# Context decay sums from high and low parts, both token tiles in one product; up tiles wait for high weights first

## The chip, the cores and the metric

The kernel runs on one core of a Trainium2 chip. The metric is device time in microseconds (us) of one execution. A core has five engines with instruction queues of their own, each worked off in order: TensorE (PE; its weight loads are shown apart as PEld), VectorE (DVE), ScalarE (ACT), GpSimd (POOL) and SyncE (SP, here only a DMA queue). They meet through semaphores: an instruction adds to one when it is done, and a `wait_ge` in another engine's program holds that engine until the count is there.

## The reference, cut to what matters

The program is one layer of a hybrid transformer (attention beside gated linear attention, GLA, then an MLP) followed by a second layer (mLSTM mixer, MLP, gated embedding), for 256 tokens of width 1024. The change touches one small piece of mathematics, the state that the 256 context tokens leave for GLA, and one waiting point in the MLPs:

```python
def gla_log_decay(lowrank, w_gk, b_gk):
    g = jax.nn.log_sigmoid((lowrank @ w_gk + b_gk).astype(jnp.float32)) / GLA_GATE_NORM
    return gla_heads(g, GLA_DK)

def gla_final_state(k, v, g):
    b = jnp.cumsum(g, axis=2)
    return jnp.einsum('bhtd,bhte->bhde', k * jnp.exp(b[:, :, -1:] - b), v)

s_f = gla_final_state(kgc, vgc, gfc)
s_b = gla_final_state(flip_t(kgc), flip_t(vgc), flip_t(gbc))

def sq_relu_mlp(h, w1, w2):
    return jnp.square(jax.nn.relu(h @ w1)) @ w2
```

There are 4 GLA heads of key width 128, 256 context tokens (two tiles of 128), and a forward and a backward direction. `b_last - b` is a sum of the decays of all later tokens (earlier ones for the backward direction), so it is a product with a strict triangle of ones.

## The kernel before, in words

All large weights arrive as 278 units of 128 x 1024 numbers in a ring of four buffers (`raw`). ACT rounds each unit to fp32r, the "high part" (`w_hi`, L1392, semaphore `hi_done`); DVE subtracts it from the original, the "low part" (`w_lo`, L1911, semaphore `unit_cut`, waited for by `wait_cut`). Activations are split the same way, and a product is three fp32r matmuls: low times high, high times high, high times low (`product`, L796). A weight tile is four units.

The order of the work is written out by hand in three plans. A plan is one list of steps, and every engine walks through the whole list and issues its own part of each step. `woven(tile, side)` lays the eight pieces of a tile's matmuls (six matmuls each in this part) beside side steps; the steps `round` (ACT) and `cut` (DVE) split the next tile's units in between. In tiles `aq1` and `ga0` the order is: piece, `round` 0, `gstate 0`; piece, keys' rotary part 2, `cut` 0; piece, `round` 1, `gstate 1`; piece, `round` 2, keys' part 3, `cut` 1; piece, `gstate 2`, `cut` 2; piece, `round` 3, keys' part 4; piece, `gstate 3`, `cut` 3; piece, queries' part 0; two pieces of `ga0`, `gstate 4`; two more pieces, `gstate 5`. The rotary parts (`rope_keys`, `rope_queries`, L2135 to L2198) are DVE's.

`gla_state(j)` is the `gstate` step, a pipeline over the four heads h:

- PE: `out` of head j-2 (L1005, decayed keys times values), then `cum` of head j-1 (L1017 and L1019, the triangle sums, plain fp32 matmuls into bank 5), then the gate product of head j (L1033).
- ACT: the copy of head j-2's state (L1566), the exponential of head j-1's sums (L1573), then Abs, Exp, Ln of head j's gate (L1558 to L1560).
- DVE: the product with the keys of head j-1 (L2231, semaphore `gs_kd`), then `min(x, 0) - log` of head j (L2236, semaphore `gs_g`), which ends that head's log decays in `gs_a`.

So DVE finishes the decays of head h in step `gstate h`, and PE sums them in step `gstate h+1`, waiting for `gs_g` alone.

The MLPs (tags `a` and `b`) run eight steps each of `up` and `down` tiles. `up` (L1163, L1166) does, for each bank, eight matmuls with the high weights (512 columns: high and low activations side by side) and then eight with the low weights (256 columns). For the first bank it waits, before every second of the high matmuls, for the unit's low part (`wait_cut`).

Of the kernel before, what the change touches and what calls it, by code (L numbers as in the profile page):

```python
# [24 lines left out]
P = 128  # L25
# [362 lines left out]
QK_BLOCKS = (tuple(zip(range(4), (7, 6, 4, 5))), ((4, 7), (5, 6)))  # L388
ROOT_ON_POOL = ("n2",)
SCALED_LATER = ("n3", "n4", "n5")  # L390
AWAKE = {}
# [8 lines left out]
def build(nc, a, out):  # L400
    with ExitStack() as ctx:
# [39 lines left out]
        diag_block = sb("diag_block", [P, 32])  # L441
        gx_c = sb("gx_c", [P, 2, 2, 32])
        gx_more = sb("gx_more", [P, N_LVL - 3, 2 * T])
        stat = sb("stat", [P, 8, 16])
# [129 lines left out]
        def head_of(name, h):  # L574
# [35 lines left out]
        go_sig, gomul_done, sig_ready = sem("go_sig"), sem("gomul_done"), sem("sig_ready")  # L610
        gs_mm, gs_ln, gs_g, gs_cum, gs_exp, gs_kd, gs_out, gs_copy = (
            sem(n) for n in ("gs_mm", "gs_ln", "gs_g", "gs_cum", "gs_exp", "gs_kd", "gs_out", "gs_copy"))
        gx_mm, gx_ln, gx_g, gx_scan, gx_eq, gx_qin = (
# [9 lines left out]
        res_ready = sem("res_ready")  # L623
        hid_done, relu_done, hid_half, hid_sum, hsq_done, hhi_done, hlo_done = (
            sem(n) for n in ("hid_done", "relu_done", "hid_half", "hid_sum", "hsq_done", "hhi_done", "hlo_done"))
        down_done, acc_done = sem("down_done"), sem("acc_done")
# [5 lines left out]
                             "mg_mt", "mg_md", "mg_em"))  # L632
        pick_zero = sem("pick_zero")
        pick_ready, mg_hi, mg_lo, mh_bc, mh_arg, mh_exp, mh_s, mh_sd, mh_num, mh_out = (
# [3 lines left out]
        sq_out, out_scale, x_gained = sem("sq_out"), sem("out_scale"), sem("x_gained")  # L638
        mean_ready, root_set = sem("mean_ready"), sem("root_set")
        block = ctx.enter_context(nc.Block())  # L640
# [98 lines left out]
        def _(pool):  # L739
# [9 lines left out]

            pool.memset(pick[:, :], 0.0).then_inc(pick_zero, 1)  # L750
            pool.memset(pick_r[:, :].bitcast(F32), 0.0).then_inc(pick_zero, 1)
            wait_cut(pool, UNIT["gk", 3])
# [6 lines left out]
            for target, name in ((qk_row[:, 0, :], "q_norm"), (qk_row[:, 1, :], "k_norm"), (gate_row[:, :], "b_gates")):  # L759
                pool.dma_start(target, a[name].partition_broadcast(P)).then_inc(params_in, 16)  # L760
            pool.wait_ge(ot_done, N_ATT)
            root = stat[:, 2, 15:16]
            pool.memset(root, -0.5).then_inc(root_set, 1)
            for r in range(4):
# [3 lines left out]
            pool.dma_start(p_in, a["p_t"]).then_inc(small_in, 16)  # L768
            pool.wait_ge(root_set, 1)
            for name in ROOT_ON_POOL:  # L770
# [17 lines left out]
        def _(pe):  # L788
# [205 lines left out]
            def gla_state(j):  # L994


                h = j - 2
                if 0 <= h < GH:
                    pe.wait_ge(gs_kd, h + 1)
                    pe.wait_ge(evac_act, EVAC["gv0" if h < 2 else "gv1", 3][1])  # L1000
                    if h >= 1:
                        pe.wait_ge(gs_copy, h)
                    for d in range(2):
                        for t in range(2):
                            last = pe.matmul(psum[6][:, d * DV:(d + 1) * DV], gs_b[:, t, d, :],  # L1005
                                             gv[:, 2 + t, h * DV:(h + 1) * DV], start=(t == 0), stop=(t == 1))
                    last.then_inc(gs_out, 1)
                h = j - 1
                if 0 <= h < GH:
                    pe.wait_ge(gs_g, h + 1)  # L1010
                    if h >= 1:
                        pe.wait_ge(gs_exp, h)

                    for d, tri, summed in ((0, l_strict, 0), (1, u_strict, 1)):
                        for t in range(2):
                            o = psum[5][:, (2 * t + d) * P:(2 * t + d + 1) * P]
                            last = pe.matmul(o, tri, gs_a[:, t, d, :], start=True, stop=(t != summed))  # L1017
                            if t == summed:
                                last = pe.matmul(o, ones, gs_a[:, 1 - t, d, :], start=False, stop=True)  # L1019
                    last.then_inc(gs_cum, 1)  # L1020
                h = j
                if 0 < h < GH:
                    pe.wait_ge(gs_g, h)
                    gla_context_gate(h)
# [122 lines left out]
            def up(tag, i, c):  # L1147


                first = UNIT_AT[tag + "u1"] - 8  # L1150
                ts = SPLIT_AT[tag + "u1"] % 2
                for g in range(2):
                    if not (isinstance(i, int) and i < 2):
                        pe.wait_ge(hid_sum, 2 * i + (SUM0[tag] + g - 3))
                    elif g == 1:
                        pe.wait_ge(relu_done, 2 * "ab".index(tag) + 2)
                    for b in range(2):
                        col = slice((2 * g + b) * P, (2 * g + b + 1) * P)
                        o = up_banks(g)[:, b]
                        for k in range(KC):  # L1160
                            if g == 0 and b == 0 and k % 2 == 0:
                                wait_cut(pe, 8 * i + (first + k // 2))
                            pe.matmul(o.rearrange("p (v t) -> p v t", v=2), w_hi[:, ts, k, col], act[:, k, 0],  # L1163
                                      start=(k == 0), stop=False, skip_group_check=True)
                        for k in range(KC):
                            last = pe.matmul(o[:, 0:T], w_lo[:, ts, k, col], act_hi[:, k, 0:T], start=False,  # L1166
                                             stop=(k == KC - 1), skip_group_check=True)
                    last.then_inc(hid_done, 1)
# [209 lines left out]
        def _(act):  # L1378
# [182 lines left out]

            def gla_state(j):
                h = j - 2
                if 0 <= h < GH:
                    act.wait_ge(gs_out, h + 1)
                    act.activation(state_of(h), psum[6][:, :].rearrange("p (d e) -> p d e", d=2),  # L1566
                                   ACT.Copy).then_inc(gs_copy, 1)
                h = j - 1
                if 0 <= h < GH:
                    act.wait_ge(gs_cum, h + 1)  # L1570
                    if h >= 1:
                        act.wait_ge(gs_out, h)
                    act.activation(gs_b.rearrange("p t d n -> p (t d n)"), psum[5][:, :], ACT.Exp,  # L1573
                                   scale=1.0 / GATE_NORM).then_inc(gs_exp, 1)
                h = j
                if 0 < h < GH:
                    gla_context_gate(h)

            def gla_context_gate(h):

                act.wait_ge(gs_mm, h + 1)
                log1p_exp(gs_a.rearrange("p t d n -> p (t d n)"), psum[4][:, :], gs_ln, h)

            def gla_gate(h):
# [113 lines left out]
            def first_hidden(tag):  # L1698

                for g in range(2):  # L1700
                    act.wait_ge(hid_done, UP0[tag] + g + 1)
                    if tag == "b":
                        act.wait_ge(hsq_done, UP0[tag] + g - 1)
                    act.activation(hid_r[:, g], psum[4 + g], ACT.Relu).then_inc(relu_done, 1)  # L1704

            def halves(tag, i):

                for g in range(2):
                    act.wait_ge(hid_done, 2 * i + (UP0[tag] + g + 1))
                    act.wait_ge(hsq_done, 2 * i + (UP0[tag] + g - 1))  # L1710
                    act.activation(hid_r[:, g].rearrange("p (b t) -> p b t", b=2), up_banks(g)[:, :, T:2 * T],  # L1711
                                   ACT.Copy).then_inc(hid_half, 1)

# [61 lines left out]
            for step in PLAN1 + [("mlp", "a")] + PLAN2 + [("mlp", "b")] + PLAN3:  # L1775
# [33 lines left out]
                elif kind == "prepare":  # L1809
# [4 lines left out]
                    hi_part(gate_x[6 * RANK:GATE_K], signs).then_inc(small_hi_done, 1)  # L1814
                    act.wait_ge(pick_zero, 2)
                    hi_part(pick_r[0:32, :], ident[0:32, 0:GH]).then_inc(pick_ready, 1)
# [84 lines left out]
        def _(dve):  # L1901
# [324 lines left out]
            def gla_state(j):  # L2226
                h = j - 1
                if 0 <= h < GH:
                    dve.wait_ge(gs_exp, h + 1)
                    keys = gk_ctx[:, :, h * HD:(h + 1) * HD].unsqueeze(2).broadcast_to([P, 2, 2, HD])  # L2230
# [119 lines left out]
            def add_halves(tag, i):  # L2350

                for g in range(2):
                    dve.wait_ge(hid_half, 2 * i + (SUM0[tag] + g - 1))
                    x = hid_r[:, g].rearrange("p (b t) -> p b t", b=2)
# [7 lines left out]
            def square(tag, i):  # L2362

                for g in range(2):
                    if isinstance(i, int) and i == 0:
                        dve.wait_ge(relu_done, 2 * "ab".index(tag) + g + 1)
                    else:
# [170 lines left out]
            for step in PLAN1 + [("mlp", "a")] + PLAN2 + [("mlp", "b")] + PLAN3:  # L2538
# [20 lines left out]
                elif kind == "prepare":  # L2559
# [4 lines left out]
                            mg_w[:, :, 0:16]).then_inc(small_lo_done, 1)  # L2564
                    dve.wait_ge(pick_zero, 1)
                    dve.tensor_tensor(pick[0:32, :], ident[0:32, 0:16], ident[0:32, 16:32], ALU.add).then_inc(pick_ready, 1)
# [192 lines left out]
```

## Time and profile before

| | us |
|---|---|
| three runs | 883.03, 884.46, 884.60 (median 884.46) |
| the profiled execution, its own time | 884.47 |
| its span (first to last instruction) | 882.7 |
| PE busy | 861.5 |
| DVE busy | 639.0 |
| ACT busy | 495.2 |
| POOL busy | 13.3 |

The span is from the first to the last instruction that the profiler saw; 1.8 us of the execution's time lie around it. Matmul ends are modelled, so two matmuls in a row are read by the distance of their starts; a plain fp32 matmul shows as two records. In a timeline a row may merge several instructions (x6), and its "us" then runs from the start of the first to the end of the last.

### The profile page before, as it was taken

How to read it: one execution, taken by the hardware profiler on the slowest of the kernel's cores; microseconds unless marked ns; L12 is line 12 of the kernel's file. 1: busy time of each engine (PE TensorE's matmuls, PEld its weight loads, DVE VectorE, ACT ScalarE, POOL GpSimd, SP SyncE). 2: the span in 40 equal slices, each digit the busy share in tenths (PEclk: the TensorE clock that was granted, in tenths of full speed). 3: DMA queues.
4: the chain of work that ended last, by engine and by line, in shares of the span. 5: the costliest groups of instructions: out<-in, count | busy, mean ns of one | idle time of the engine just before them, and what ended most of it. 6: DMA issues, size and time to landing. Idle time of an engine off the chain costs nothing.

```text
span 882.7 us, 14095 instructions
## 1 busy us (share of the span) xinstructions
PE 861.5 (98%) x5072; PEld 723.9 (82%) x5072; DVE 639.0 (72%) x1014; ACT 495.2 (56%) x802; POOL 13.3 (2%) x28
## 2 busy tenths in 40 slices
PE   5999999999999999999999999999999999999996
PEld 2888888887788888888888888988888788888885
DVE  3479998888879878776555568767777855555575
ACT  4586787756575665474444444453755544444554
POOL 0020000000000000000000000000000000000001
PEclk9999999999999999999999999999999999999998
DMA  9853333335447776736555558353443765555531
GB/s 363 357 160 120 120 113 133 115 120 191 143 156 269 267 260 206 237 117 208 191 197 189 189 189 271 102 192 133 143 130 135 265 241 190 190 193 193 169 130 48
DMA packets 45265, 161.89 MB, mean 183 GB/s; under 512 B 5500, under 2 KB 5660, under 8 KB 45216
## 3 DMA queue, kind: packets, MB, share of 16 engines
q1 hardware_dynamic: 43200, 156.78, 52.0%
q0 software_dynamic: 1296, 3.78, 1.5%
q8 instruction: 33, 0.54, 0.3%
q10 hardware_dynamic: 720, 0.65, 0.2%
q14 instruction: 16, 0.13, 0.0%
HBM read 160.15 MB, written 1.05 MB: 183 GB/s over the span
## 4 chain that ended last, share of the span: by engine, by line
PE 77%; DVE 12%; ACT 6%; issue 4%; DMA 1%; SPq 0%; POOL 0%; POOLq 0%; ACTq 0%; DVEq 0%
PE bank L796 47%; PE bank L1163 12%; PE bank L1166 6%; DVE w_lo L1911 3%; PE bank L984 1%; DVE arena L2297 1%; ACT w_hi L1392 1%; PE bank L974 1%; DMA arena<-in_early 1%; ACT gx_more L1624 1%; PE bank L1288 1%; DVE small L1941 1%; PE bank L1097 1%; PE bank L1102 1%; ACT arena L1477 1%
## 5 line engine op out<-in xcount | busy, mean ns | idle before, releaser
L796 PE MATMUL bank<-w_hi,act 128*128 128x512 f32 (+1 forms) x1456 | 453.9, 393 | 0.3 <-DVE w_lo L1911 0.2
L1911 DVE TENSOR_TENSOR w_lo<-raw,w_hi 128x1024 fp32r<-128x1024 f32 x244 | 288.2, 1220 | 58.6 <-ACT w_hi L1392 57.7
L796 PEld LDWEIGHTS bank<-w_hi,act 128*128 128x128 f32 x1456 | 267.0, 188 | 54.6 <-issue 2.4
L796 PE MATMUL bank<-w_lo,act 128*128 128x512 f32 (+1 forms) x728 | 282.4, 388 | 0.0
L1392 ACT ACTIVATE w_hi<-raw 128x1024 fp32r<-128x1024 f32 x244 | 245.3, 1051 | 60.2 <-PE bank L796 41.7
L796 PEld LDWEIGHTS bank<-w_lo,act 128*128 128x128 f32 x728 | 136.7, 188 | 28.8
L1163 PE MATMUL bank<-act,w_hi 128*128 128x512 f32 x448 | 112.5, 392 | 0.8 <-DVE w_lo L1911 0.8
L1163 PEld LDWEIGHTS bank<-act,w_hi 128*128 128x128 f32 x448 | 81.1, 189 | 16.7 <-DVE w_lo L1911 1.9
L1392 ACT ACTIVATE act<-arena 128x512 fp32r<-128x512 f32 (+1 forms) x65 | 39.5, 630 | 63.7 <-DVE arena L2369 33.4
L796 PE MATMUL bank<-act,w_hi 128*128 128x256 f32 x384 | 72.7, 290 | 2.4 <-DVE act L1911 1.8
L2355 DVE TENSOR_TENSOR arena<-bank,arena 128x512 f32<-128x512 f32 x28 | 19.3, 691 | 65.2 <-ACT arena L1711 65.2
L1711 ACT ACTIVATE arena<-bank 128x512 f32<-128x512 f32 x28 | 16.8, 598 | 87.9 <-PE bank L1166 87.9
L796 PEld LDWEIGHTS bank<-act,w_hi 128*128 128x128 f32 x384 | 60.4, 194 | 5.6 <-DVE act L1911 3.8
L1166 PEld LDWEIGHTS bank<-act,w_lo 128*128 128x128 f32 x448 | 61.1, 190 | 4.4
L1166 PE MATMUL bank<-act,w_lo 128*128 128x256 f32 x448 | 62.5, 282 | 0.0
L796 PE MATMUL bank<-act,w_lo 128*128 128x256 f32 x192 | 54.7, 285 | 0.0
L1911 DVE TENSOR_TENSOR act<-arena,act 128x512 fp32r<-128x512 f32 (+1 forms) x65 | 42.6, 688 | 6.9 <-ACT act L1392 6.2
L1941 DVE SCALAR_TENSOR_TENSOR small<-raw,silu_c,small 128x512 f32<-128x512 f32 x56 | 42.0, 750 | 4.1 <-DMA raw<-in_stream 2.3
L796 PEld LDWEIGHTS bank<-act,w_lo 128*128 128x128 f32 x192 | 37.3, 194 | 0.0
L1463 ACT ACTIVATE arena<-bank 128x512 f32<-128x512 f32 x42 | 24.6, 589 | 8.9 <-PE bank L796 8.7
L984 PEld LDWEIGHTS bank<-arena 128*128 128x128 f32 x128 | 16.7, 191 | 7.2 <-issue 5.7
L2369 DVE SCALAR_TENSOR_TENSOR arena<-arena 128x512 f32<-128x512 f32 x32 | 20.7, 686 | 2.3 <-ACT arena L1704 2.2
(272 smaller groups left out, 736.9 us busy)
## 6 DMA issues: line engine op xcount, KB each, us to landing
raw<-in_stream SPq DMA_DIRECT2D x278, 512.0 KB, 4.3
arena<-in_early SPq DMA_DIRECT2D x16, 512.0 KB, 10.8
res<-in_x SPq DMA_DIRECT2D x2, 512.0 KB, 4.2
arena<-in_ctx SPq DMA_DIRECT2D x2, 512.0 KB, 10.0
res<-in_x POOLq DMA_DIRECT2D x1, 1024.0 KB, 7.5
arena<-in_norm_final POOLq DMA_DIRECT2D x1, 512.0 KB, 4.1
arena<-in_ple_b POOLq DMA_DIRECT2D x1, 512.0 KB, 5.0
out<-arena ACTq DMA_DIRECT2D x2, 256.0 KB, 2.6
```

Source lines behind the costliest of these rows:

```text
L796: last = pe.matmul(o, left, right, start=start and m == 0, stop=stop and m == 2, skip_group_check=shared)
L974: pe.matmul(psum[4 + i % 2][:, :], q_t[:, h, t * P:(t + 1) * P], k_t[:, h // (QH // KVH), :], start=True, stop=True).then_inc(score_done, 1)
L984: last = pe.matmul(psum[7][:, t * P:(t + 1) * P], kv[:, c, c0:c0 + HD], prob_t[:, c, :], start=(c == 0), stop=(c == 3))
L1163: pe.matmul(o.rearrange("p (v t) -> p v t", v=2), w_hi[:, ts, k, col], act[:, k, 0], start=(k == 0), stop=False, skip_group_check=True)
L1166: last = pe.matmul(o[:, 0:T], w_lo[:, ts, k, col], act_hi[:, k, 0:T], start=False, stop=(k == KC - 1), skip_group_check=True)
L1392: return act.activation(o, i, ACT.Copy)
L1463: act.activation(o, i, ACT.Copy, scale=scale).then_inc(evac_act, 1)
L1711: act.activation(hid_r[:, g].rearrange("p (b t) -> p b t", b=2), up_banks(g)[:, :, T:2 * T], ACT.Copy).then_inc(hid_half, 1)
L1911: return dve.tensor_tensor(o, x, hi.bitcast(F32), ALU.subtract)
L1941: ins = dve.scalar_tensor_tensor(out=ada_sum, in0=w, scalar=c, in1=ada_sum, op0=ALU.mult, op1=ALU.add)
L2355: dve.tensor_tensor(x, up_banks(g)[:, :, 0:T], x, ALU.add).then_inc(hid_sum, 1)
L2369: dve.scalar_tensor_tensor(out=hid_h[:, g], in0=hid_r[:, g], scalar=0.0, in1=hid_r[:, g], op0=ALU.max, op1=ALU.mult).then_inc(hsq_done, 1)
```

## The change

In the context state, each head's decays `gs_a` are split into a high part (ACT, `gs_hi`) and a low part (DVE, `gs_lo`), as the weights are. The two strict triangles and the ones matrix are rounded to fp32r once, by POOL. The sums become eight fp32r matmuls a head (per direction: triangle times high and times low over both token tiles at once, 256 columns; ones times high and times low of the one other tile, 128 columns) in place of six plain fp32 ones. The new tiles take the memory of `gx_more`, so POOL's rounding waits for the last level product. PE waits for `gs_lo_done` in place of `gs_g`; ACT's split stands at the start of its `gla_state(h+1)`, DVE's subtraction at the start of its own.

In `up`, the first bank's high matmuls wait for `hi_done` of their unit, and `wait_cut` moves ahead of the low matmuls of the same chunk. Some semaphores are merged under one name (`relu_done` and `hid_half` into `hid_read`, `pick_zero` and `root_set` into `pool_done`) with the same points in the order.

```diff
+        with nc.sbuf_tensor("later_r", [P, 2 * NC + 3 * P], F32R) as later_r:
+            gs_hi, gs_lo = (later_r[:, i * NC:(i + 1) * NC].rearrange("p (t d n) -> p t d n", t=2, d=2) for i in range(2))
+            u_strict_r, l_strict_r, ones_r = (later_r[:, 2 * NC + i * P:2 * NC + (i + 1) * P] for i in range(3))
         gx_more = sb("gx_more", [P, N_LVL - 3, 2 * T])
...
+            pool.wait_ge(lv_mm, len(BATCHES) * GH)
+            pool.wait_ge(params_in, 16 * N_PARAMS)
+            pool.tensor_copy(later_r[:, 2 * NC:2 * NC + 2 * P], consts[:, 1:3, :].rearrange("p m n -> p (m n)")).then_inc(pool_done, 1)
+            pool.tensor_copy(ones_r, ones).then_inc(pool_done, 1)
...
                 h = j - 1
                 if 0 <= h < GH:
-                    pe.wait_ge(gs_g, h + 1)
+                    pe.wait_ge(gs_lo_done, h + 1)
                     if h >= 1:
                         pe.wait_ge(gs_exp, h)
-
-                    for d, tri, summed in ((0, l_strict, 0), (1, u_strict, 1)):
-                        for t in range(2):
-                            o = psum[5][:, (2 * t + d) * P:(2 * t + d + 1) * P]
-                            last = pe.matmul(o, tri, gs_a[:, t, d, :], start=True, stop=(t != summed))
-                            if t == summed:
-                                last = pe.matmul(o, ones, gs_a[:, 1 - t, d, :], start=False, stop=True)
+                    else:
+                        pe.wait_ge(pool_done, TRI_SET)
+                    sums = psum[5][:, :].rearrange("p (t d n) -> p t d n", t=2, d=2)
+                    for d, tri, summed in ((0, l_strict_r, 0), (1, u_strict_r, 1)):
+                        pe.matmul(sums[:, :, d], tri, gs_hi[:, :, d], start=True, stop=False, skip_group_check=True)
+                        pe.matmul(sums[:, :, d], tri, gs_lo[:, :, d], start=False, stop=False, skip_group_check=True)
+                        pe.matmul(sums[:, summed, d], ones_r, gs_hi[:, 1 - summed, d], start=False, stop=False,
+                                  skip_group_check=True)
+                        last = pe.matmul(sums[:, summed, d], ones_r, gs_lo[:, 1 - summed, d], start=False, stop=True,
+                                         skip_group_check=True)
                     last.then_inc(gs_cum, 1)
...
                         for k in range(KC):
                             if g == 0 and b == 0 and k % 2 == 0:
-                                wait_cut(pe, 8 * i + (first + k // 2))
+                                pe.wait_ge(hi_done, 8 * i + (HI_AT[tag + "u1", k // 2] - 7))
                             pe.matmul(o.rearrange("p (v t) -> p v t", v=2), w_hi[:, ts, k, col], act[:, k, 0],
                                       start=(k == 0), stop=False, skip_group_check=True)
                         for k in range(KC):
+                            if g == 0 and b == 0 and k % 2 == 0:
+                                wait_cut(pe, 8 * i + (first + k // 2))
                             last = pe.matmul(o[:, 0:T], w_lo[:, ts, k, col], act_hi[:, k, 0:T], start=False,
...
             def gla_state(j):
+                if 0 <= j - 1 < GH:
+                    gla_context_hi(j - 1)
...
+            def gla_context_hi(h):
+
+                act.wait_ge(gs_g, h + 1)
+                hi_part(gs_hi, gs_a).then_inc(gs_hi_done, 1)
...
             def gla_state(j):
                 h = j - 1
                 if 0 <= h < GH:
+                    dve.wait_ge(gs_hi_done, h + 1)
+                    lo_part(gs_lo, gs_a, gs_hi).then_inc(gs_lo_done, 1)
                     dve.wait_ge(gs_exp, h + 1)
```

## Rows read from the trace of the kernel before

**Rows 1.** The page's part 1: busy us, share of the span, instructions of each engine.
```profile
PE 861.5 (98%) x5072; PEld 723.9 (82%) x5072; DVE 639.0 (72%) x1014; ACT 495.2 (56%) x802; POOL 13.3 (2%) x28
```
**Rows 2.** Timeline of PE: start us, us, what, count; gate, `cum` and `out`.
```profile
153.81 0.40 PE L1033 MATMUL bank<-gate_r 98*128 98x256 f32 x2
...
159.52 0.38 PE L1017 MATMUL bank<-arena,consts 128*128 128x128 f32 x2
...
159.96 0.83 PE L1017 MATMUL bank<-arena,consts 128*128 128x128 f32 x6
160.63 0.39 PE L1019 MATMUL bank<-arena,consts 128*128 128x128 f32 x2
...
163.84 1.89 PE L1005 MATMUL bank<-arena 128*128 128x256 f32 x8
165.56 0.38 PE L1017 MATMUL bank<-arena,consts 128*128 128x128 f32 x2
...
169.91 1.89 PE L1005 MATMUL bank<-arena 128*128 128x256 f32 x8
...
177.35 1.89 PE L1005 MATMUL bank<-arena 128*128 128x256 f32 x8
```
**Rows 3.** Timeline of DVE over these steps; in brackets idle time before and its releaser.
```profile
161.35 1.22 DVE L1911 TENSOR_TENSOR w_lo<-raw,w_hi 128x1024 fp32r<-128x1024 f32 x1
162.49 0.68 DVE L2231 TENSOR_TENSOR arena<-arena 128x512 f32<-128x512 f32 x1
163.50 0.69 DVE L2236 SCALAR_TENSOR_TENSOR arena<-bank,arena 128x512 f32<-128x512 f32 x1 [0.33 <-ACT arena L1560]
...
166.34 1.23 DVE L1911 TENSOR_TENSOR w_lo<-raw,w_hi 128x1024 fp32r<-128x1024 f32 x1
...
169.55 0.69 DVE L2236 SCALAR_TENSOR_TENSOR arena<-bank,arena 128x512 f32<-128x512 f32 x1 [1.12 <-ACT arena L1560]
...
172.54 0.42 DVE L2146 TENSOR_TENSOR arena<-arena,rows 128x256 f32<-128x256 f32 x1
...
175.62 0.69 DVE L2236 SCALAR_TENSOR_TENSOR arena<-bank,arena 128x512 f32<-128x512 f32 x1 [1.12 <-ACT arena L1560]
...
178.22 1.28 DVE L2182 TENSOR_REDUCE stat<-arena 128x4 f32<-128x512 f32 x2
181.31 0.69 DVE L2231 TENSOR_TENSOR arena<-arena 128x512 f32<-128x512 f32 x1 [1.81 <-ACT arena L1573]
```
**Rows 4.** Timeline of ACT: the exponential of head 0's sums, and head 1's Ln.
```profile
161.05 0.60 ACT L1573 ACTIVATE arena<-bank 128x512 f32<-128x512 f32 x1 [0.48 <-PE bank L1019]
...
162.84 0.63 ACT L1560 ACTIVATE arena<-arena 128x512 f32<-128x512 f32 x1
```
**Rows 5.** Busy by stretch: stretch, us, PE, PEld, DVE, ACT, POOL, clock, DMA.
```profile
151.40:162.50 11.10, 11.10 (x59) 9.45 (x58) 10.55 (x26) 7.60 (x16) 0.00 (x0) 1.00 0.46 143
...
190.00:212.00 22.00, 22.00 (x111) 16.89 (x109) 21.31 (x44) 13.04 (x25) 0.00 (x0) 1.00 0.66 210
```
**Rows 6.** Timeline of PE: matmuls of 16 columns with a 128x128 weight.
```profile
570.38 0.52 PE L1226 MATMUL bank<-pick,arena 128*128 128x16 f32 x4
```
**Rows 7.** Timeline of POOL: the one operation on a wide tile.
```profile
868.88 1.29 POOL L781 TENSOR_TENSOR arena<-res,arena 128x512 f32<-128x512 f32 x1 [148.78 <-DVE res L2124]
```
**Rows 8.** Timeline of PE: first `up` tile of the second MLP.
```profile
683.61 1.13 PE L1163 MATMUL bank<-act,w_hi 128*128 128x512 f32 x4
685.15 0.73 PE L1163 MATMUL bank<-act,w_hi 128*128 128x512 f32 x2 [0.40 <-DVE w_lo L1911]
...
686.86 1.12 PE L1166 MATMUL bank<-act,w_lo 128*128 128x256 f32 x8
```
**Rows 9.** Timeline of DVE: the low parts of that tile's four units.
```profile
681.59 4.63 DVE L1911 TENSOR_TENSOR w_lo<-raw,w_hi 128x1024 fp32r<-128x1024 f32 x4 [0.42 <-DVE stat L2390]
```
**Rows 10.** Busy by stretch near the start (columns as in rows 5).
```profile
14.17:17.58 3.41, 1.49 (x18) 0.45 (x18) 2.87 (x7) 1.20 (x2) 0.00 (x0) 1.00 1.03 411
17.58:21.00 3.42, 3.42 (x20) 2.60 (x20) 1.23 (x1) 1.06 (x1) 0.00 (x0) 0.50 1.02 407
```

More of the change, by code:

```diff
@@ L389 @@
 ROOT_ON_POOL = ("n2",)
+TRI_SET = 4
+ROOT_SET = 5
 SCALED_LATER = ("n3", "n4", "n5")
@@ L610, in build @@
         go_sig, gomul_done, sig_ready = sem("go_sig"), sem("gomul_done"), sem("sig_ready")
-        gs_mm, gs_ln, gs_g, gs_cum, gs_exp, gs_kd, gs_out, gs_copy = (
-            sem(n) for n in ("gs_mm", "gs_ln", "gs_g", "gs_cum", "gs_exp", "gs_kd", "gs_out", "gs_copy"))
+        gs_mm, gs_ln, gs_g, gs_hi_done, gs_lo_done, gs_cum, gs_exp, gs_kd, gs_out, gs_copy = (
+            sem(n) for n in ("gs_mm", "gs_ln", "gs_g", "gs_hi_done", "gs_lo_done", "gs_cum", "gs_exp", "gs_kd", "gs_out",
+                             "gs_copy"))
         gx_mm, gx_ln, gx_g, gx_scan, gx_eq, gx_qin = (
@@ L623, in build @@
         res_ready = sem("res_ready")
-        hid_done, relu_done, hid_half, hid_sum, hsq_done, hhi_done, hlo_done = (
-            sem(n) for n in ("hid_done", "relu_done", "hid_half", "hid_sum", "hsq_done", "hhi_done", "hlo_done"))
+        hid_done, hid_read, hid_sum, hsq_done, hhi_done, hlo_done = (
+            sem(n) for n in ("hid_done", "hid_read", "hid_sum", "hsq_done", "hhi_done", "hlo_done"))
         down_done, acc_done = sem("down_done"), sem("acc_done")
@@ L632, in build @@
                              "mg_mt", "mg_md", "mg_em"))
-        pick_zero = sem("pick_zero")
         pick_ready, mg_hi, mg_lo, mh_bc, mh_arg, mh_exp, mh_s, mh_sd, mh_num, mh_out = (
@@ L638, in build @@
         sq_out, out_scale, x_gained = sem("sq_out"), sem("out_scale"), sem("x_gained")
-        mean_ready, root_set = sem("mean_ready"), sem("root_set")
+        mean_ready, pool_done = sem("mean_ready"), sem("pool_done")
         block = ctx.enter_context(nc.Block())
@@ L748, in cuts @@
                                            w_hi[:, SPLIT_AT[n] % 2, at].bitcast(F32), ALU.subtract).then_inc(unit_cut, 1)
-            pool.memset(pick[:, :], 0.0).then_inc(pick_zero, 1)
-            pool.memset(pick_r[:, :].bitcast(F32), 0.0).then_inc(pick_zero, 1)
+            pool.memset(pick[:, :], 0.0).then_inc(pool_done, 1)
+            pool.memset(pick_r[:, :].bitcast(F32), 0.0).then_inc(pool_done, 1)
             wait_cut(pool, UNIT["gk", 3])
@@ L760, in _ @@
                 pool.dma_start(target, a[name].partition_broadcast(P)).then_inc(params_in, 16)
+            pool.wait_ge(lv_mm, len(BATCHES) * GH)
+            pool.wait_ge(params_in, 16 * N_PARAMS)
+            pool.tensor_copy(later_r[:, 2 * NC:2 * NC + 2 * P], consts[:, 1:3, :].rearrange("p m n -> p (m n)")).then_inc(pool_done, 1)
+            pool.tensor_copy(ones_r, ones).then_inc(pool_done, 1)
             pool.wait_ge(ot_done, N_ATT)
             root = stat[:, 2, 15:16]
-            pool.memset(root, -0.5).then_inc(root_set, 1)
+            pool.memset(root, -0.5).then_inc(pool_done, 1)
             for r in range(4):
@@ L768, in _ @@
             pool.dma_start(p_in, a["p_t"]).then_inc(small_in, 16)
-            pool.wait_ge(root_set, 1)
+            pool.wait_ge(pool_done, ROOT_SET)
             for name in ROOT_ON_POOL:
@@ L1155, in up @@
                     elif g == 1:
-                        pe.wait_ge(relu_done, 2 * "ab".index(tag) + 2)
+                        pe.wait_ge(hid_read, UP0[tag] + 2)
                     for b in range(2):
@@ L1703, in first_hidden @@
                         act.wait_ge(hsq_done, UP0[tag] + g - 1)
-                    act.activation(hid_r[:, g], psum[4 + g], ACT.Relu).then_inc(relu_done, 1)
+                    act.activation(hid_r[:, g], psum[4 + g], ACT.Relu).then_inc(hid_read, 1)
             def halves(tag, i):
@@ L1711, in halves @@
                     act.activation(hid_r[:, g].rearrange("p (b t) -> p b t", b=2), up_banks(g)[:, :, T:2 * T],
-                                   ACT.Copy).then_inc(hid_half, 1)
+                                   ACT.Copy).then_inc(hid_read, 1)
             def mlp(tag, name):
@@ L1814, in _ @@
                     hi_part(gate_x[6 * RANK:GATE_K], signs).then_inc(small_hi_done, 1)
-                    act.wait_ge(pick_zero, 2)
+                    act.wait_ge(pool_done, 2)
                     hi_part(pick_r[0:32, :], ident[0:32, 0:GH]).then_inc(pick_ready, 1)
@@ L2352, in add_halves @@
                 for g in range(2):
-                    dve.wait_ge(hid_half, 2 * i + (SUM0[tag] + g - 1))
+                    dve.wait_ge(hid_read, 2 * i + (UP0[tag] + g + 1))
                     x = hid_r[:, g].rearrange("p (b t) -> p b t", b=2)
@@ L2365, in square @@
                     if isinstance(i, int) and i == 0:
-                        dve.wait_ge(relu_done, 2 * "ab".index(tag) + g + 1)
+                        dve.wait_ge(hid_read, UP0[tag] + g + 1)
                     else:
@@ L2564, in _ @@
                             mg_w[:, :, 0:16]).then_inc(small_lo_done, 1)
-                    dve.wait_ge(pick_zero, 1)
+                    dve.wait_ge(pool_done, 1)
                     dve.tensor_tensor(pick[0:32, :], ident[0:32, 0:16], ident[0:32, 16:32], ALU.add).then_inc(pick_ready, 1)
```

## The prediction

> **What bounds the kernel now.** I read the page's busy shares first: PE works 861.5 of 882.7 us [rows 1], so the end is set by PE, and anything that makes PE stand still is paid nearly in full. Then I read the stretch that the change touches in the timelines of PE, DVE and ACT side by side. What the reader should see there is who is ahead. PE does the first `cum` at 159.52 [rows 2]; that is step `gstate 1`. DVE comes to its own part of `gstate 1`, the product with the keys, at 162.49, straight behind `cut` 0 at 161.35 [rows 3]. It waits for nobody there: between 151.40 and 162.50 it works 10.55 of 11.10 us [rows 5]. So DVE is 3 us behind PE in the list of steps. Today that is harmless, since `cum` needs only `gs_g`, which DVE issues one step earlier.
>
> **Part 1, the sums themselves.** Out go twelve records a head. Eight of them, from 159.96 on, start 0.67/6 = 0.112 us apart [rows 2], so 12 x 0.112 = 1.34 us. In come four products of 256 columns and four of 128. A 256-column fp32r product costs (1.12 - 0.28)/7 = 0.12, with 0.28 for the last one's modelled length [rows 8]. No row has an fp32r product of 128 columns. From below it is bounded by the column rate, half of 0.12, 0.06; from above by the price of a plain one, two records, 0.22. I take 0.11, because even 16 columns past a fresh 128x128 weight start about 0.11 apart ((0.52 - 0.17)/3, [rows 6]), as if the weight load set the pace. New `cum`: 4 x 0.12 + 4 x 0.11 = 0.92, saving 0.42 a head, 1.68 in all; with the bounds 1.68 + 0.8 = 2.5 or 1.68 - 1.76 = -0.1.
>
> The Trainium skill, page "TensorE: Matmul & The Clock Gate", section "Back-to-back issue gap", gives about 81 ns for a weight load and matmul pair of 128 columns; no run here shows it, and by it, as an estimate, the total would be 16 x 0.03 = 0.5 us lower, 890.7.
>
> **Part 2, the wait.** PE now waits in `gstate h+1` for a subtraction that DVE does in that same step, while it waited for one from the step before. Behind the waiting matmul stand all later pieces of `aq1` and `ga0`. ACT's rounding costs 0.60 (its other 512-column operations, [rows 4]) and lies in ACT's gaps: for head 0 it fits in the 0.48 idle and runs out at about 161.2, before DVE asks. DVE's subtraction costs 0.69 as its neighbours of that size [rows 3]. Allow 0.07 for the signal to PE.
>
> Head 0: DVE subtracts from 162.49; `cum` can start at 162.49 + 0.69 + 0.07 = 163.25. PE is there at 159.52. Stall 3.73.
>
> What hangs on `cum`: before, the next head's decays (L2236) started 163.50 - 159.52 = 3.98 after it, through gate, Abs, Exp and Ln, with no slack (0.33 idle, released by Ln, [rows 3, 4]). With the shorter `cum` this is 3.56. The chain then goes round: DVE's decays, DVE's own rotary work and cut, subtraction, PE.
>
> Head 1: decays start at 163.25 + 3.56 = 166.81. From there to the end of `cut` 1 took 166.34 - 163.50 + 1.14 = 3.98 (1.14 is the distance of a cut to what follows it, 161.35 to 162.49) [rows 3], so 170.79; plus 0.76 gives 171.55. PE arrives, from 163.25, after 163.84 - 159.52 - 0.42 = 3.90 at `out`, and 165.56 - 163.84 = 1.72 later at `cum` [rows 2]: 168.87. Stall 2.68.
>
> Head 2: decays at 171.55 + 3.56 = 175.11; `cut` 2 and keys' part 4 took 172.96 - 169.55 = 3.41 [rows 3]: 178.52, plus 0.76 is 179.28. PE arrives at 171.55 + (169.91 - 165.56 - 0.42) + 1.72 = 177.20 [rows 2]. Stall 2.08.
>
> Head 3: decays at 182.84; `cut` 3 and queries' part 0 took 179.50 - 175.62 = 3.88 [rows 3]: 186.72, plus 0.76 is 187.48. PE's last `cum` before was at 171.63 and the next `out` at 177.35, 5.72 later [rows 2], so it arrives at 179.28 + 5.72 - 0.42 + 1.72 = 186.30. Stall 1.18.
>
> Sum 3.73 + 2.68 + 2.08 + 1.18 = 9.67, less the saving 1.68: +7.99. The idle time that DVE had before each decay and before the last key product (1.12, 1.12, 1.81, [rows 3]) is used up in this sum already; that is why the stalls shrink.
>
> Does the time come back? After `gstate 5` DVE is the close follower: 21.31 of 22.00 us busy from 190 to 212 [rows 5]. Its work after the last exponential is moved by what moved that exponential, which is what moved PE, so both shift alike, and PE meets no long wait later that a head start of DVE could fill.
>
> POOL's two roundings wait for the last level products, which are done before PE's first gate product at 153.81, since that waits for what is made of them [rows 2]; even at 1.29 each [rows 7] they end by 156.4, 3 us before 159.52. Nothing. If they were three times slower they would still lie under the first stall. The merged semaphores keep their points: nothing.
>
> **Part 3, `up`.** Only the first `up` tile of the second MLP shows a wait for low parts: its eight high matmuls take from 683.61 to 686.86 [rows 8]. Unhindered they take 8 x 0.235 = 1.88 (0.235 between the 0.227 of clean ones and the 0.243 of the four in the row), to 685.49. The low parts of all units end at 681.59 + 4.63 = 686.22 [rows 9]; the low matmul of the last unit's first chunk is due at 685.49 + 6 x 0.12 = 686.21, so 0.07 stays. The high parts exist before DVE starts on a unit, so that wait costs nothing. Gain 686.86 - 685.49 - 0.07 = 1.30 (between 0 and 1.4). What then follows on ACT and DVE waits for PE anyhow. All other `up` tiles gain nothing.
>
> **Sum.** The profiled execution took 884.47 (span 882.7 and 1.8 around it), and the median of the three runs is 884.46, so nothing is to be converted. 884.47 + 7.99 - 1.30 = 891.2.
>
> **Rivals.**
> *The low part is there in time.* If DVE began the subtraction of head 0 before 158.76 (159.52 less 0.76), and so for each head, no stall would come and both gains would show: 884.47 - 1.68 - 1.30 = 881.5. For it: DVE has idle time of 1.1 to 1.8 us in these steps. Against: that idle time lies behind ACT's Ln and exponential, not before the subtraction, and for head 0 there is none; DVE would have to come 3.7 us earlier. It is decided at DVE's place in the list of steps.
>
> *Only the first stall is paid.* Once PE is 3.7 us later, DVE might no longer be behind: 884.47 + 3.73 - 2.98 = 885.2. Against: DVE's next decays hang on PE's gate product, behind the stalled `cum`, so it is set back as well.
>
> *The clock falls in a stall.* Near the start PE worked 1.49 of 3.41 us, and in the 3.42 us after that the clock was 0.50, 1.2 in place of 2.4 GHz, with work worth 1.71 us lost [rows 10]. The first stall leaves PE idle about as long. One such stretch gives 891.2 + 1.7 = 892.9 at most, two give 894.6; part of it would lie under the next stall, where DVE is late anyway. The Trainium skill has this rule too (same page, section "Part 1: The HAM clock gate (the "warmup" mystery)"): an idle TensorE is set back to half its clock; the trace agrees in the stretch just named.
>
> *128 columns of fp32r at 0.22.* Each head's `cum` would be 0.44 longer, and it lies in the chain that goes round: +1.76, 892.9.
>
> **Chances.** Forecast 0.65, with a range of its own of 890 to 892.3 (the 128-column bound below, 0.1 either way in the signal times per head, 0 to 1.4 for `up`); low part in time 0.05; first stall only 0.08; clock 0.15; dear 128 columns 0.07. Measurements of this kernel tell 0.2% from no change, 1.8 us: 882.7 to 886.2 is "the same". So faster 0.06, the same 0.08, slower 0.86. Range 888.0 to 893.5: it takes in the forecast, one clock stretch and the dear columns, and leaves out the two low cases and two clock stretches.
>
> **What would show it.** In the trace after, PE idle before the first matmul of each `cum`, released by DVE's write of the low part, about 3.7, 2.7, 2.1 and 1.2 us long; `cum` taking 0.9; the key product of head 3 about 8 us later than 181.31 and the rest of the kernel shifted by the same 8 until 684; PE's 0.40 waits in that `up` tile gone, and the shift after it 6.7. It would be wrong if those waits are under 1 us, if the shift shrinks between 190 and 680, or if the granted clock shows 0.5 between 160 and 190.

## The result and the profile after

The changed kernel takes 890.11 us (median of six, 889.29 to 891.13) against 883.98 for the kernel before (median of six): ratio 1.0075, 95% interval 1.0064 to 1.0085 (the plain quotient of the two medians is 1.0069), slower by 6.1 us by the medians. The forecast was slower, 891.2, in 888.0 to 893.5. The profiled execution took 891.13 (span 889.3), against 884.47 (882.7): 6.7 more.

Who PE waited for in the profile after (us in total, times, longest); the second row is new, the third is as in the kernel before, and the 0.8 us of waits in `up` are gone:

```profile
PE bank L1324 <- DMA arena<-in_early: 8.0, 3, 7.6
PE bank L1026 <- DVE later_r L1932: 7.2, 4, 3.5
PE bank L805 <- DVE act L1932: 1.8, 2, 1.6
```

The timeline of PE after (L1026 to L1030 are `cum`, L1014 `out`, L1045 the gate product), which answers to [rows 2]:

```profile
153.85 0.40 PE L1045 MATMUL bank<-gate_r 98*128 98x256 f32 x2
...
159.33 0.39 PE L805 MATMUL bank<-w_lo,act 128*128 128x512 f32 x1
163.27 0.39 PE L1026 MATMUL bank<-later_r 128*128 128x256 f32 x1 [3.55 <-DVE later_r L1932]
163.49 0.28 PE L1027 MATMUL bank<-later_r 128*128 128x256 f32 x1
163.61 0.22 PE L1028 MATMUL bank<-later_r 128*128 128x128 f32 x1
163.66 0.28 PE L1030 MATMUL bank<-later_r 128*128 128x128 f32 x1
163.78 0.33 PE L1026 MATMUL bank<-later_r 128*128 128x256 f32 x1
...
164.24 0.46 PE L1045 MATMUL bank<-gate_r 98*128 98x256 f32 x2
164.53 0.71 PE L805 MATMUL bank<-w_hi,act 128*128 128x512 f32 x2
...
168.88 1.89 PE L1014 MATMUL bank<-arena 128*128 128x256 f32 x8
171.61 0.39 PE L1026 MATMUL bank<-later_r 128*128 128x256 f32 x1 [0.84 <-DVE later_r L1932]
...
175.62 1.89 PE L1014 MATMUL bank<-arena 128*128 128x256 f32 x8
179.30 0.39 PE L1026 MATMUL bank<-later_r 128*128 128x256 f32 x1 [1.80 <-DVE later_r L1932]
...
184.68 1.89 PE L1014 MATMUL bank<-arena 128*128 128x256 f32 x8
187.58 0.39 PE L1026 MATMUL bank<-later_r 128*128 128x256 f32 x1 [1.02 <-DVE later_r L1932]
...
191.36 1.89 PE L1014 MATMUL bank<-arena 128*128 128x256 f32 x8
```

The four `cum` start at 163.27, 171.61, 179.30 and 187.58; the prediction had 163.25, 171.55, 179.28 and 187.48. The timeline of DVE, which answers to [rows 3]: the new subtraction (`later_r`) stands behind `cut` 0 and `cut` 1, and PE starts 0.06 us after it ends.

```profile
161.39 1.22 DVE L1932 TENSOR_TENSOR w_lo<-raw,w_hi 128x1024 fp32r<-128x1024 f32 x1
162.53 0.68 DVE L1932 TENSOR_TENSOR later_r<-arena,later_r 128x512 fp32r<-128x512 f32 x1
165.07 0.69 DVE L2254 TENSOR_TENSOR arena<-arena 128x512 f32<-128x512 f32 x1 [1.86 <-ACT arena L1589]
166.88 0.69 DVE L2259 SCALAR_TENSOR_TENSOR arena<-bank,arena 128x512 f32<-128x512 f32 x1 [1.12 <-ACT arena L1574]
...
169.73 1.23 DVE L1932 TENSOR_TENSOR w_lo<-raw,w_hi 128x1024 fp32r<-128x1024 f32 x1
170.87 0.68 DVE L1932 TENSOR_TENSOR later_r<-arena,later_r 128x512 fp32r<-128x512 f32 x1
```

ACT and POOL were early, as their timelines show; neither is what `cum` waited for. ACT's roundings for the other heads start at 168.18, 176.05 and 185.26, and DVE's subtractions at 170.87, 178.56 and 186.84. The rows of ACT and of POOL:

```profile
160.52 0.62 ACT L1406 ACTIVATE later_r<-arena 128x512 fp32r<-128x512 f32 x1
```
```profile
146.59 0.40 POOL L768 CAST later_r<-consts 128x256 fp32r<-128x256 f32 x1 [97.00 <-PE bank L1092]
146.93 0.29 POOL L769 CAST later_r<-consts 128x128 fp32r<-128x128 f32 x1
```

The `up` tile, PE and then DVE, which answers to [rows 8, 9]: eight high matmuls without a gap, 693.39 - 691.55 = 1.84 us, not 3.25.

```profile
691.55 2.00 PE L1175 MATMUL bank<-act,w_hi 128*128 128x512 f32 x8
693.39 1.11 PE L1180 MATMUL bank<-act,w_lo 128*128 128x256 f32 x8
```
```profile
689.16 4.63 DVE L1932 TENSOR_TENSOR w_lo<-raw,w_hi 128x1024 fp32r<-128x1024 f32 x4
```

One thing was not in the sum: the clock. Busy time by stretch (columns as in [rows 5]), before, in and after the stretch at 0.50:

```profile
161.50:164.90 3.40, 1.63 (x12) 1.59 (x13) 1.71 (x2) 0.46 (x1) 0.00 (x0) 1.00 0.27 86
165.00:168.30 3.30, 3.30 (x9) 2.58 (x8) 2.08 (x4) 3.24 (x7) 0.00 (x0) 0.50 0.16 63
168.40:171.80 3.40, 2.56 (x12) 1.90 (x11) 3.08 (x6) 1.00 (x2) 0.00 (x0) 1.00 0.00 0
```

### The profile page after: what moved, and what is told of

The parts are those of the page before. It is cut to its first block, busy times and chain, and to the rows that moved or that the text cites. A ratio compares the mean times of both kernels' runs of the same rounds, so it can differ in the third digit from the quotient of the medians.

```text
span 889.3 us, 14123 instructions
## 1 busy us (share of the span) xinstructions
PE 861.8 (97%) x5056; PEld 723.6 (81%) x5056; DVE 641.1 (72%) x1018; ACT 496.9 (56%) x806; POOL 13.9 (2%) x30
## 3 DMA queue, kind: packets, MB, share of 16 engines
q0 software_dynamic: 1296, 3.78, 1.5%
## 4 chain that ended last, share of the span: by engine, by line
PE 74%; DVE 14%; ACT 7%; issue 4%; DMA 1%; SPq 0%; POOL 0%; POOLq 0%; ACTq 0%; DVEq 0%
PE bank L805 46%; PE bank L1175 12%; PE bank L1180 6%; DVE w_lo L1932 3%; PE bank L993 1%; ACT w_hi L1406 1%; DVE arena L2320 1%; PE bank L983 1%; DMA arena<-in_early 1%; ACT gx_more L1645 1%; PE bank L1302 1%; DVE small L1962 1%; PE bank L1109 1%; PE bank L1114 1%; PE bank L1324 1%
```

## The experiments

Times are medians; "there" is the kernel before on the same chip, run beside it. The ratios with their intervals are not the quotients of the two medians. To place the time I measured three distances in each trace, which do not depend on how the start went: from head 0's gate product (153.81 in the kernel before) to head 3's `out` (183.19), from there to the first `up` matmul of the second MLP (683.61), and from that to its first low matmul (the column "`up` high").

| kernel | median | there | ratio (95%) | gate 0 to out 3 | to `up` | `up` high |
|---|---|---|---|---|---|---|
| before | 883.98 | | | 29.38 | 500.42 | 3.25 |
| changed | 890.11 | 883.98 | 1.0075 (1.0064-1.0085) | 37.51 | 500.19 | 1.84 |
| after_again | 890.39 | 883.08 | 1.0080 (1.0066-1.0093) | 37.50 | 500.17 | 1.84 |
| up_only | 882.76 | 882.93 | 0.9990 (0.9981-0.9999) | 29.38 | 500.24 | 1.84 |
| up_only_again | 881.72 | 882.78 | 0.9985 (0.9976-0.9994) | 29.38 | 500.30 | 1.84 |
| sums_only | 890.49 | 882.93 | 1.0075 (1.0061-1.0089) | 38.40 | 500.13 | 2.88 |
| wait_only | 894.13 | 882.93 | 1.0120 (1.0105-1.0136) | 40.63 | 500.24 | 2.88 |
| low_early | 883.84 | 882.93 | 1.0000 (0.9991-1.0009) | 30.62 | 500.24 | 1.84 |
| low_pool | 883.99 | 883.08 | 1.0010 (1.0001-1.0019) | 31.60 | 500.22 | 1.84 |
| low_pool_spread | 883.97 | 883.08 | 1.0012 (1.0003-1.0021) | 34.59 | 497.26 | 1.84 |
| low_early_spread | 886.33 | 883.08 | 1.0034 (1.0023-1.0045) | 36.01 | 497.15 | 1.84 |
| low_early_placed | 882.91 | 882.78 | 1.0002 (0.9993-1.0011) | 28.54 | 502.33 | 1.84 |

The medians alone mislead where a difference is 1 or 2 us. The executions of one kernel fall into two groups about 1.6 us apart, and their mean granted clock tells them apart: those of the kernel before with 0.997 or 0.998 have medians of 882.5 to 882.9 in the three sets, the others 884.3 to 884.5. The kept traces show the difference as one stretch of 3.4 us at 0.50 near 18 us ([rows 10] has it, up_only's trace has not). Group against group, without and with that stretch, the differences from the kernel before are: up_only -1.2 and -1.2, up_only_again -0.9 and -1.2, low_early +0.1 and -0.2, low_early_placed +0.3 and -0.2, low_pool +1.0 and +0.9, low_pool_spread +0.9 and +0.8, low_early_spread +1.7 (a single execution) and +1.9. Some of these groups have only three to five executions.

**The parts alone: up_only and sums_only.** The kernel before with only the new waiting point, and the changed kernel with the old one. The edit of up_only; that of sums_only is the same lines the other way round:

```diff
-                                wait_cut(pe, 8 * i + (first + k // 2))
+                                pe.wait_ge(hi_done, 8 * i + (HI_AT[tag + "u1", k // 2] - 7))
...
+                            if g == 0 and b == 0 and k % 2 == 0:
+                                wait_cut(pe, 8 * i + (first + k // 2))
```

> The kernel before with the waiting point of the MLPs' up tiles alone. My theory (every idle time of PE is paid in full, and the first up tile of the second MLP held about 1.3 of it): 884.0 - 1.3 = 882.7, both 0.40 us waits gone. Rival (the gain is given back, since ACT and DVE behind it are late next): 884.0, with a new wait of PE within the next few us.

> The changed kernel with the old waiting point in the up tiles: the sums alone. My theory: the shift of the changed kernel at 684 us, 7.9, stays to the end: 884.0 + 7.5 = 891.5 (the changed kernel's 890.1 and the 1.4 of the up tile). Rival (the head start that DVE and ACT get while PE stands is used later, the changed kernel's up tile then gained less): under 890.5.

Alone the new point gives 1.41 us at its tile in the trace, and group against group about 1.2 of it reaches the end; the medians give 0.2 and 1.1, ratio intervals just under 1, because 6 of 11 executions of the one run and 3 of 11 of the other have the stretch near 18 us. sums_only carries the whole loss. In it the old point costs 2.88 where it cost 3.25 before, and 1.84 is the least, so on top of the new sums the point is worth 1.04: DVE starts on that tile's units 2.4 us ahead of PE after the change (689.16, 691.55) and was 2.0 ahead before, for a reason that I did not follow up. By the medians sums_only (890.49) cannot be told from the changed kernel beside its own kernel before; my 891.5 was 1.0 high.

**The wait without the cheaper sums: wait_only.** sums_only with the six plain products put back:

```diff
-                        pe.matmul(sums[:, :, d], tri, gs_hi[:, :, d], start=True, stop=False, skip_group_check=True)
-                        pe.matmul(sums[:, :, d], tri, gs_lo[:, :, d], start=False, stop=False, skip_group_check=True)
...
+                            last = pe.matmul(o, tri, gs_a[:, t, d, :], start=True, stop=(t != summed))
+                            if t == summed:
+                                last = pe.matmul(o, ones, gs_a[:, 1 - t, d, :], start=False, stop=True)
```

> As sums_only, but PE sums with the six plain fp32 products of before: the split is made and waited for, and not used. My theory (the waits are the loss, the cheaper products a gain of 0.4 a head that lies in the chain going round): four waits of about 3.7, 2.7, 2.1 and 1.2 again, and a longer cum, 1.5 to 1.7 above sums_only: 893.2. Rival (the new products are no cheaper in the chain): equal to sums_only.

The four waits are there; in the timeline of PE (the first records of the four `cum`):

```profile
161.92 0.49 PE L1027 MATMUL bank<-arena,consts 128*128 128x128 f32 x2 [3.52 <-DVE later_r L1928]
...
170.73 0.79 PE L1027 MATMUL bank<-arena,consts 128*128 128x128 f32 x2 [2.48 <-DVE later_r L1928]
...
180.21 0.49 PE L1027 MATMUL bank<-arena,consts 128*128 128x128 f32 x2 [1.73 <-DVE later_r L1928]
...
188.96 0.49 PE L1027 MATMUL bank<-arena,consts 128*128 128x128 f32 x2 [1.07 <-DVE later_r L1928]
```

By the medians it is 3.6 us above sums_only, not 1.6, and by the distances of the traces 2.2 (40.63 against 38.40), where sums_only has lost 0.9 to the clock. The cheaper products do pay, but not all of the difference is theirs: here the clock was at 0.50 from 170.4 to 173.7, just as head 1's `cum` ran, so it lay in the chain that goes round. How much is theirs these two runs do not separate.

**The same work in another place: low_early.** ACT's rounding and DVE's subtraction move from the start of step `gstate h+1` to the end of `gstate h`. DVE's new lines:

```diff
                     dve.scalar_tensor_tensor(out=flat, in0=psum[4][:, :], scalar=0.0, in1=flat, op0=ALU.min,
                                              op1=ALU.subtract).then_inc(gs_g, 1)
+                    dve.wait_ge(gs_hi_done, h + 1)
+                    lo_part(gs_lo, gs_a, gs_hi).then_inc(gs_lo_done, 1)
```

> The changed kernel with ACT's and DVE's split of head h moved from step gstate h+1 to the end of step gstate h, straight behind the decays; nothing else differs. My theory (the loss is DVE's place in the list, not the work of the split): PE's wait before the first sums falls from 3.5 to about 1.4 (ACT rounds after the unit of round 0), about 1.2 and 0.3 for heads 1 and 2 and none for head 3: 884.0 + 2.9 - 1.7 - 1.4 = 883.8. Rival (the added work on DVE and ACT is the loss): it stays near 890.

This decides between the theories: with the same instructions this stretch is 1.2 us longer than in the kernel before (30.62 against 29.38), not 8.1. In the timeline of PE there are two waits left. The waits that were expected for heads 1 and 2 are not there. One that is left is for ACT's rounding behind round 0, as expected, and one that I had not seen, `out` waiting for the key product, since DVE had stood 1.9 us for ACT:

```profile
160.77 0.39 PE L1026 MATMUL bank<-later_r 128*128 128x256 f32 x1 [1.21 <-DVE later_r L1932]
...
165.56 1.99 PE L1014 MATMUL bank<-arena 128*128 128x256 f32 x8 [0.62 <-DVE arena L2252]
```
```profile
160.02 0.69 DVE L1932 TENSOR_TENSOR later_r<-arena,later_r 128x512 fp32r<-128x512 f32 x1 [1.88 <-ACT later_r L1406]
```

**The changed kernel again: after_again.**

> The changed kernel once more, beside its variants on one chip: the ratio 1.0075 again. The stretch from head 0's gate product to head 3's out (29.4 us in the kernel before, 37.5 in the first trace of the changed one) stays between 37.2 and 38.5; if TensorE's clock falls in a stretch where DVE is late anyway it costs nothing, else up to 1.7.

The loss repeats, and the distance to 0.01 us, with the clock at 0.50 from 162.4 to 165.7. Only one of its five executions is without the stretch near 18 us, so its 7.3 us by the medians is too much: the other four have a median of 890.4, 5.9 above the kernel before with the stretch.

**POOL makes the low parts: low_pool, low_pool_spread.** low_early with the subtraction on POOL and `gstate 0` ahead of the keys' part 1; in the second kernel the steps `gstate 2` to `5` also stand further apart. The lists shown are the second kernel's:

```diff
+            for h in range(GH):
+                pool.wait_ge(gs_hi_done, h + 1)
+                pool.tensor_tensor(gs_lo, gs_a, gs_hi.bitcast(F32), ALU.subtract).then_inc(gs_lo_done, 1)
...
+    p.woven("aq0", lv[c:] + [("gsfirst",), k[0], gs[0], k[1]])
+    p.woven("aq1", [None, k[2], gs[1], k[3], None, gs[2], k[4], q[0]])
+    p.woven("ga0", [gs[3], q[1], None, gs[4], None, gs[5] , [q[2], ("qkturn", 0)], q[3]])
```

> As low_early, but POOL makes the low parts, ACT rounds at the end of step gstate h, and gstate 0 stands before the keys' part 1 (so head 0's decays are there 0.8 us earlier, before ACT's round 0). My theory: no wait before head 0's sums, 0.7 to 1.1 us each for heads 1 and 2 (POOL needs 1.3 for what DVE does in 0.7), none for head 3: kernel before - 1.7 - 1.4 + 1.8 = kernel before - 1.3. Rival (POOL's work slows DVE, or DVE's new place of gstate 0 does): kernel before or slower.

> As low_pool, with steps gstate 2 to 5 moved later in the lists of aq1 and ga0 so that three pieces of matmuls, not two, lie between the sums of two heads. My theory: no wait before any sums, the stretch from gate 0 to head 3's out is shorter by 1.7 at equal matmuls, total: kernel before - 3.0. Rival (DVE becomes late for the attention that follows, where it is 97% busy): a wait of PE for the scores or probabilities of 1 to 3 us near 212, total near the kernel before.

Both missed by 2 to 4 us. In low_pool the rival held. In low_pool_spread the rival's total held, but not its place: PE waits 1.9 us for POOL's low parts and 1.4 for key products inside the stretch, and none over 0.3 us near 212. In low_pool PE waits for DVE's key product instead:

```profile
164.00 1.99 PE L1017 MATMUL bank<-arena 128*128 128x256 f32 x8 [1.83 <-DVE arena L2255]
166.61 0.39 PE L1029 MATMUL bank<-later_r 128*128 128x256 f32 x1 [0.62 <-POOL later_r L772]
```

Its DVE and POOL timelines show one reason: the DVE operation that meets POOL's takes 1.50 in place of 0.42.

```profile
155.41 0.42 DVE L2159 TENSOR_TENSOR arena<-arena 128x256 f32<-128x256 f32 x1
...
156.31 1.50 DVE L2159 TENSOR_TENSOR arena<-arena 128x256 f32<-128x256 f32 x1
```
```profile
156.24 1.29 POOL L772 TENSOR_TENSOR later_r<-arena,later_r 128x512 fp32r<-128x512 f32 x1 [10.46 <-ACT later_r L1409]
```

It happened at each of the four (1.47, 1.49 and 1.51 at 165.37, 171.98 and 178.61). So work given to POOL was work put on DVE, and the later place of the key product in DVE's time met PE's `out`. In the spread form the second distance is 3 us shorter because two steps of the list have changed sides of the mark, so only the sum of the two tells: 531.85, against 531.82 in low_pool. In the kernel before it is 529.80. Spreading gained nothing.

**The spread with DVE: low_early_spread.**

> As low_pool_spread, but DVE makes the low parts straight behind the decays, so it waits 0.7 us for ACT each time. My theory: DVE carries 4 x 0.7 of work and 4 x 0.7 of waiting more; its idle time in the stretch before, 5.3 us, covers most: up to 1 us slower than low_pool_spread, kernel before - 2.3. Rival (DVE's added time shows in full near 212): kernel before + 1 to 2.

886.33, 3.3 above its kernel before by the medians and 1.7 to 1.9 group against group, as only one of its seven executions is without the stretch near 18 us. The expectation missed; the rival's size came, but not where it had put it. PE waits 3.2 us in three places for the key products (0.8, 0.5, 1.9), 1.1 for a low part and nothing near 212; DVE was late inside the stretch already.

**DVE's other work behind the chain: low_early_placed.**

```diff
+    p.woven("aq0", lv[c:] + [("gsfirst",), k[0], k[1], gs[0]])
...
+    p.steps += [a1[0], r[0], a1[1], k[2], a1[2], r[1], gs[1], a1[3], r[2], cu[0], cu[1], ("evac", "aq1", 0)]
...
+    p.steps += [a1[4], gs[2], a1[5], r[3], cu[2], k[3], a1[6], gs[3], a1[7], cu[3], k[4], ("evac", "aq1", 1)]
+    p.woven("ga0", [gs[4], [q[0], q[1]], gs[5], None, q[2], ("qkturn", 0), q[3]])
```

> low_early with DVE's other work put behind the chain: gstate 0 ahead of ACT's evacuation and round 0, cuts 0 and 1 and the keys' part 3 after gstate 1 and 2, queries' part 0 after gstate 4; PE's order is the same. My theory: no wait of PE over 0.3 us in steps gstate 1 to 4, so gate 0 to head 3's out is 27.7 to 28.5 us (29.4 before, 30.6 in low_early); but DVE, with 4 x 0.7 of work and about as much waiting more, is then the late one, and PE waits 1 to 2 us for it near 212: total kernel before - 1.4 to - 2. Rival A (nothing is late at 212): kernel before - 3. Rival B (DVE cannot be placed so that the chain is free): waits stay, total at or above kernel before.

The stretch is now shorter than in the kernel before, 28.54 against 29.38: the cheaper products show at last. But the distance after it grew by 1.9 (502.33 against 500.42), in waits for DVE that no other kernel has:

```profile
188.63 1.94 PE L974 MATMUL bank<-consts,arena 128*128 128x128 f32 x16 [0.31 <-DVE arena L2225]
197.46 1.09 PE L974 MATMUL bank<-consts,arena 128*128 128x128 f32 x8 [0.29 <-DVE arena L2225]
208.60 0.66 PE L1006 MATMUL bank<-consts,arena 128*128 128x128 f32 x4 [0.60 <-DVE arena L2250]
```

These come to 1.2 of the 1.9; the rest I could not put to single rows. DVE is the late one after the stretch, as I expected, though from 188 on and not only near 212; the total (882.91 against 882.78) is 1.5 to 2.1 worse than forecast.

**The version that beats both: up_only_again.**

> The kernel before with the up tiles' waiting point alone, once more, as the mark for low_early_placed on the same chip: kernel before - 1.2 (its first high matmul to its first low one 1.84 us, not 3.25).

881.72 against 882.78, ratio 0.9985. Of all forms tried, the kernel before with only the new waiting point is the fastest.

## Why the prediction was right

*The wait.* The mechanism is shown: low_early has the same instructions in another place of ACT's and DVE's lists and its stretch is 1.2 us longer than before, not 8.1. By the timeline after, the delays ahead of the four `cum` are 3.71 (159.56 to 163.27), 2.62, 1.96 and 1.18, against stalls of 3.73, 2.68, 2.08 and 1.18 forecast. The second is not all a wait: 1.61 of it is what the matmuls ahead took longer at 0.50 (164.53 to 168.88 took 4.35, in the kernel before 2.74), and PE then stood for the last 1.01. The chain went round as forecast: a head's decays start 3.61 to 3.63 after its predecessor's `cum`, where the sum had 3.56.

*The sums.* This term was mis-sized. From start to start, the four products of 256 columns take 0.22, 0.12, 0.17 and 0.12, 0.63 where I had 0.48, and the four of 128 columns 0.05 or 0.06 and 0.12 or 0.11 in turn, 0.34 where I had 0.44 (163.27 to the gate product at 164.24, 0.97 in all, forecast 0.92). The old `cum` I had put too high: from 159.52 to its gate product at 160.77 it takes 1.25, not 1.34. With 0.05 more that the matmuls behind it gain, a head saves 0.32 to 0.34, not 0.42: from a `cum` to the next `out` it is 4.35 before and 4.01 after for head 1, 5.71 and 5.38 for head 2, 4.12 and 3.78 for head 3. That is 1.33 in all, forecast 1.68. Delays of 9.47 less 1.33 are 8.14; the distance grew by 8.13, forecast 7.99. The stalls were forecast 0.20 too long and the saving 0.35 too large, so part of the closeness of the sum is two errors that offset each other.

*Nothing comes back.* Right: 500.19 after the stretch, 500.42 before; 0.2 us returned.

*`up`.* 1.41 in place of 1.30 by the trace: the eight high matmuls take 1.84 and not 1.88, and the 0.07 that I had left for the last low part did not come, as DVE was 0.4 us further ahead. Beside the new sums 1.04 of it remains.

*The clock.* This rival I gave 0.15 as a case of its own at up to +1.7. It did come, in every trace with the 3.5 us wait (four of four), and so did the sign that the prediction had named for being wrong, a granted clock of 0.50 between 160 and 190 (164.9 to 168.3). In wait_only it came only with the second wait, from 170.4, and not behind the first. In the changed kernel it cost nothing: after the time lost PE still had 1.01 us to stand for DVE, as one clause of the rival said, and both its traces, at 0.50 in different places, have 37.5. Where it fell on the chain it cost: in sums_only it begins at 162.2, inside head 0's `cum`, and the next `cum` starts 8.91 after this one (161.81 to 170.72) where the changed kernel has 8.34; a second stretch, from 179.3 to 182.6, brings its distance to 38.40, 0.9 more in all. wait_only has 40.63 against 39.05 by the prediction's own sum with the plain products. So the rival was real and its price in this kernel mis-sized: near zero where DVE was late anyway, 0.6 and 1.6 where it lay on the chain. The forecast of 891.2 has no such stretch in it; that it fell in both traces where it cost nothing is luck.

*The level.* 891.2 was built on a profiled execution of 884.47 with a stretch at 0.50 near its start [rows 10]; executions of the kernel before lie near 882.7 without it and 884.4 with it (told apart by their mean granted clock; no kept trace of this kernel is without it), so a median moves by up to 1.7 with how many of them have it. By their times, two of the three executions that the forecast was built on have it, and three of the six behind 883.98. That is most of the 1.1 us between 890.11 and 891.2: the profiled execution after has such a stretch too, and took 891.13.

## What to carry to other kernels

When a producer's step is added to a list that several engines walk in order, ask where in its own time that engine stands when the consumer gets there, not how long the step is: four DVE operations of 0.7 us cost 8 us here. Read it off the two timelines at the same step; a lag that is harmless today, because the consumer asks for something a step older, becomes a wait of that lag and the new step on top (162.53 less 159.56, and 0.68 for the subtraction, for the first head). And when the chain is then cleared, look for where the displaced work becomes the next wait.

## What the runs showed of the hardware

- A DVE operation with two operands in SBUF stood for about as long as POOL's subtraction took: 1.47 to 1.51 us in place of 0.42 beside POOL operations of 1.27 to 1.53. The Trainium skill, page "SBUF — State Buffer", section "SBUF: two separate sides", says that DVE, in an operation with two inputs in SBUF, and a GpSimd operation that reads SBUF take turns on a shared pair of ports, which the first holds for its whole instruction while the other is fully blocked. The trace agrees with its 1.1 us of blocking. POOL's cast of 256 columns took 0.40, where the only wide POOL operation of the kernel before had taken 1.29 [rows 7].
- The clock fell after stretches in which PE was partly at work, not idle: 1.63 of 3.40 us in the changed kernel, 1.49 of 3.41 in [rows 10], which the prediction had likened to PE standing still. In up_only's trace the clock did not fall at that place of the start:

```profile
14.20:17.60 3.40, 2.21 (x18) 0.59 (x18) 2.87 (x7) 1.19 (x2) 0.00 (x0) 1.00 1.02 405
17.60:21.00 3.40, 3.40 (x34) 2.39 (x33) 1.23 (x1) 1.06 (x1) 0.00 (x0) 1.00 1.03 411
```

The 2.21 is no more work than the 1.49: both have 18 matmuls, but a group of eight that takes 0.64 at 14.25 in the kernel before takes 1.08 at 14.21 in up_only, as it does in both at 8.8. So PE came to full speed later in that execution, although the clock column shows 1.00 there already. Its gate product of head 0 comes at 152.19, 1.6 us earlier than the 153.81 of the kernel before, though nothing differs between the two up to there; why one execution has the low stretch and another not, the runs do not show.
